# Making the low halves of a weight slab at the end of VectorE's round in the attention of a two-block network

## The chip, the cores and the metric

The kernel runs on one core of a Trainium2 chip. The metric is the time of one execution on the device in microseconds (us), the median of several runs.

## The reference, cut to what matters

Ten layers over 256 tokens of width 1024: feed-forward layers, a mixer, a short convolution, a shared key and value projection and a sparse attention. All is float32. Only the mixer is touched:

```
h = x @ w_in                      # 1024 -> 3 * 3 * 384 (q, k, v of three branches) + 3 * 1024 (gates)
o_m = moba_attention(...)         # 6 heads, one block here: causal softmax with ALiBi
o_d = diff_attention(...)         # 6 heads, softmax_1 - lam * softmax_2, then RMSNorm per head
o_s = stick_breaking_attention(...)   # 6 heads
gates = sigmoid(g + b_gate)
merged = gates_0 * (o_m @ w_br_moba) + gates_1 * (o_d @ w_br_diff) + gates_2 * (o_s @ w_br_sb)
out = merged @ w_out
```

## The kernel before, in words

**Slabs.** Every weight matrix comes through SBUF in slabs of 128 x 2048 float32 (1 MB; some of the mixer's are 128 x 1536) in a ring of four slots. A float32 product is made of three float32r matmuls (`product`, L1566 to L1568), so each slab is split: ScalarE copies `raw` to the rounded high half `w_hi` (L628), VectorE subtracts it from `raw` and so makes the low half `w_lo` (L974). A slab's high half waits until its load has landed and TensorE has used the slab four before it (`slab_used`); its low half waits for the high half (`high_ready`); TensorE waits for the low half (`low_ready`), and so does the load into the same slot of the slab four further on (SyncE's queue, L394).

**The mixer.** Its 36 slabs are numbered 0 to 35 here. Slabs 0 to 31 are those of 19 tiles (`TILES`), one or two slabs each. The tiles are pieces of q, k and v, six half gates (for each branch two of 512 columns) and six half branch products. Tile number t accumulates in the PSUM banks of pair t mod 2 (`pair_of`). Before TensorE begins a tile, it waits until all earlier tiles of that pair were read out (`pair_read`). The tiles that matter below: tile 6 is the second half of the first gate (slabs 12, 13), tiles 7 and 8 the first branch's products (slabs 14 and 15), tiles 9 and 10 queries, keys and values of the third branch (slabs 16 to 19), tiles 11 and 12 the second gate (20 to 23), tiles 13 and 14 the second branch's products (24 and 25), tile 15 half of the third gate (26, 27).

**Rounds.** The attention of the 18 heads (u = 0 to 17, six to a branch) is woven between the slabs by a table written out by hand; `ROUND[i]` holds the slabs of round i:

```
STEPS = [6] + [1] * 8 + [2] * 3 + [1] * 4 + [2, 1, 1] + [4]
```

So round 7 has slab 12, round 8 slab 13, round 9 slabs 14 and 15, round 10 slabs 16 and 17, round 11 slabs 18 and 19, rounds 12 to 15 slabs 20 to 23, round 16 slabs 24 and 25, rounds 17 and 18 slabs 26 and 27, round 19 the last four. Each engine runs its own loop over u in the order of its program, and in pass u works on round u + 1:

- TensorE: the slabs of round u + 1; the square sums of a pair of heads (L1817, odd passes of the second branch); the three transposes of the weights of head u (L1790, waits `prob_ready`); the scores of a head ahead; the output of head u - 1 (L1810 to L1812), which for an even u - 1 also waits until the pair of heads before it was taken out of its bank, by VectorE's L1191 or L1206.
- ScalarE: reads out q and k tiles, copies the transposed weights (L726), exponentials of head u + 1 (L717; in the third branch a logarithm chain L697 to L709), the high half of a finished pair of heads (L734), the four sigmoids of a gate whose second half was made in this round, with a table load on either side (L689, L690), and last the high halves (L628) of the slabs four after those of round u + 1.
- VectorE: reads out the round's tiles (`tiles`: v L1103, gates L1113, branch products L1125 or L1128 and L1129, each tile ended by a nop at L1115 or L1131 that counts `pair_read`), the root mean square's sum (L1191), the maxima of head u + 1 (L1144 to L1154), the weights of head u + 1 (L1174 to L1183, in the third branch L1164 to L1169), the low half of a finished pair of heads (L1206), the pair's normalisation (L1197 to L1201), and the low halves L974 of slabs.

The branch products at L1125 and L1128 multiply by the gate, so VectorE waits there for ScalarE's sigmoids (`gated`).

Of the kernel before, what the change touches and what calls it, by code (L numbers as in the profile page):

```python
# [54 lines left out]
def two_block_kernel(nc, t, out):  # L55
# [5 lines left out]
    with ExitStack() as ctx:  # L61
# [246 lines left out]
        HEADS = BRANCH_HEADS  # L308
# [17 lines left out]
        ROUND = [range(sum(STEPS[:i]), sum(STEPS[:i + 1])) for i in range(len(STEPS))]  # L326
# [60 lines left out]
        def _(sp):  # L387
# [40 lines left out]
            for n, kind in enumerate(phases):  # L428
# [33 lines left out]
                elif kind == MIXER:  # L462
                    w = t["w_in"][0]
                    for d, (tile, kh) in enumerate(MIX_SLABS):
                        what = TILES[tile]
                        if d == ROUND[0].stop:
                            gains(n)

                            sp.wait_ge(normed, normed_before(n))
                            sp.dma_start(b_gate[:], t["b_gate"][0].partition_broadcast(P)).then_inc(loaded_mix, 16)  # L470
                        if what[0] == "gate":
                            c0 = GATE0 + what[1] * D + what[2] * 512
                            load(s0 + d, columns(w, kh, [(c0, 256), (c0 + 256, 256)]))
                        elif what[0] == "branch":
                            wb = t[("w_br_moba", "w_br_diff", "w_br_sb")[what[1]]][0]
                            src = wb[:, what[2] * 512:(what[2] + 1) * 512].rearrange("(k p) n -> p k n", p=P)

                            def pieces(slot):
                                dst = raw[:, slot, 0:BC * 512].rearrange("p (k n) -> p k n", k=BC)
                                return [(dst[:, :, 0:256], src[:, :, 0:256]), (dst[:, :, 256:512], src[:, :, 256:512])]  # L480
                            load(s0 + d, pieces)
                        else:
                            spans = QKV[what[0]][0]
                            load(s0 + d, columns(w, kh, spans, sum(c for _, c in spans)))
# [134 lines left out]
        def _(act):  # L619
# [41 lines left out]
            for n, kind in enumerate(phases):  # L661
                s0 = first_slab[n]
                if kind == MIXER:
                    def tile_out(tile):

                        what = TILES[tile]
                        if what[0] in QKV:
                            _, blocks, first = QKV[what[0]]
                            act.wait_ge(slab_used, s0 + MIX_SLABS.index((tile, 1)) + 1)
                            for i in range(blocks // 2):  # L670
                                at, src = first + 2 * i, pair_of(tile)[i][:].rearrange("p (k m) -> p k m", k=2)
                                queries = min(2, max(0, 4 * BC + BC - at)) if at >= 4 * BC else 0
                                if 0 < queries < 2:
                                    nc.scalar.activation(qk[:, at:at + queries, :], src[:, 0:queries, :], ACT.Copy, scale=HD ** -0.5)
                                    at, src, queries = at + queries, src[:, queries:, :], 0

                                nc.scalar.activation(qk[:, at:first + 2 * i + 2, :], src, ACT.Copy,
                                                     scale=HD ** -0.5 if queries else 1.0).then_inc(pair_read[tile % 2], 1)
# [280 lines left out]
        def _(dve):  # L959
# [8 lines left out]
            def split(k, i=0):  # L968

                if k >= TOTAL:  # L970
                    return
                slot, width = k % SLOTS, width_of(k)
                dve.wait_ge(high_ready, k + 1 + 4 * i)
                nc.vector.tensor_tensor(w_lo[:, slot, 0:width], raw[:, slot, 0:width],  # L974
                                        w_hi[:, slot, 0:width].bitcast(F32), ALU.subtract).then_inc(low_ready, 1)
# [110 lines left out]
            for n, kind in enumerate(phases):  # L1086
                s0 = first_slab[n]
                if kind == MIXER:
# [44 lines left out]
                    def maxima_of(u):  # L1133

                        b, hd = u // HEADS, u % HEADS
                        dve.wait_ge(scored, u + 1)
                        if before(u) > 0:
                            dve.wait_ge(probT_psum, before(u))
                        scale = HD ** -0.5 if b == MOBA else DIFF_SCALE
                        slope = alibi_slope(2 * hd if b == MOBA else 2 * hd + 1)  # L1140
                        maps = 1 if b == MOBA else 2
                        for m in range(maps):
                            side = u % 2 if b == MOBA else m
                            ins = nc.vector.scalar_tensor_tensor(out=prob[:, side, :], in0=far[:], scalar=slope / scale,  # L1144
                                                                 in1=bank[4 + side][:, 0:BW], op0=ALU.mult, op1=ALU.add)
                        ins.then_inc(score_read, 1)
                        dve.wait_ge(score_read, u + 1)
                        mx = head_max[:, u % 2, 0:2 * maps]
                        for m in range(maps):
                            side = u % 2 if b == MOBA else m  # L1150
                            for i, at in enumerate((ROWS_A, ROWS_B)):
                                ins = nc.vector.tensor_reduce(head_max[:, u % 2, 2 * m + i:2 * m + i + 1], prob[:, side, at], AX.X, ALU.max)
                        step(ins)
                        nc.vector.tensor_scalar(mx, mx, -scale, None, ALU.mult).then_inc(neg_ready, 1)  # L1154
# [33 lines left out]
                    def pair_spread(p):  # L1188

                        dve.wait_ge(o_sums, p - BC + 1)  # L1190
                        nc.vector.tensor_scalar(ms_d, bank[7][:, S:2 * S], 1.0 / HD, SUBLN_EPS, ALU.mult, ALU.add).then_inc(o_spread, 1)  # L1191

                    def pair_norm(p):

                        near_one = tmp[:, 0:S]
                        dve.wait_ge(o_rstd, p - BC + 1)
                        step(nc.vector.tensor_tensor(near_one, o_root, o_root, ALU.mult))  # L1197
                        step(nc.vector.tensor_tensor(near_one, near_one, ms_d, ALU.mult))
                        step(nc.vector.tensor_scalar(near_one, near_one, -0.5, 1.5, ALU.mult, ALU.add))
                        step(nc.vector.tensor_tensor(near_one, near_one, o_root, ALU.mult))  # L1200
                        nc.vector.scalar_tensor_tensor(out=o_f, in0=o_f, scalar=out_gain, in1=near_one,  # L1201
                                                       op0=ALU.mult, op1=ALU.mult).then_inc(o_normed, 1)

                    def pair_out(p, src):
                        dve.wait_ge(oT_high, p + 1)
                        nc.vector.tensor_tensor(oT_lo[:, p % BC, :], src, oT_hi[:, p % BC, :].bitcast(F32), ALU.subtract)\  # L1206
                            .then_inc(oT_ready, 1)

                    def tiles(i):
                        for d in ROUND[i]:  # L1210
                            if ends(d) is not None:
                                tile_out(ends(d))

                    def slabs(steps):
                        for d in steps:
                            split(s0 + d + 4)
# [8 lines left out]
                    for u in range(3 * HEADS):  # L1225

                        delayed = (u - 3) // 2 if u % 2 == 1 and (u - 3) // 2 // BC == DIFF else None
                        tiles(u + 1)
                        if delayed is not None:
                            pair_spread(delayed)  # L1230
                        if u + 1 < 2 * HEADS:
                            maxima_of(u + 1)
                        if u > 0:
                            slabs(ROUND[u][:1])
                        if u + 1 < 3 * HEADS:
                            weights_of(u + 1)
                        if u > 0:
                            slabs(ROUND[u][1:])
                        if u % 2 == 0 and u > 0 and (u // 2 - 1) // BC != DIFF:
                            pair_out(u // 2 - 1, bank[7][:, 0:S])  # L1240
                        if delayed is not None:
                            pair_norm(delayed)
                            pair_out(delayed, o_f)
                    slabs(ROUND[3 * HEADS])
                    pair_out(3 * BC - 1, bank[7][:, 0:S])
                    for d in ROUND[-1]:
                        if ends(d) is not None:
# [823 lines left out]
```

## Time and profile before

| | |
|---|---|
| time, median of 3 runs | 1755.72 us (1755.58 to 1756.56) |
| the profiled execution's own time | 1758.67 us |
| its span, first to last instruction | 1757.0 us |
| mean granted TensorE clock | 0.972 |
| busy: TensorE / VectorE / ScalarE | 96% / 55% / 43% |
| the mixer's rounds in the trace | 245 to 445 us |

A timeline is read line by line: start in us, duration in us, engine, line, operation, tensor written and read, count of like instructions merged, and in brackets the idle time of that engine just ahead of it with what ended it. Matmuls overlap, so the work of TensorE is measured from start to start.

### The profile page before, as it was taken

The page shows a single profiled execution, that of the slowest core. Times are in us where ns is not written, and L with a number is a line of the kernel's source. Part 1 is how long each engine was busy: PE and PEld are TensorE (multiplying, and loading weights), DVE is VectorE, ACT ScalarE, POOL GpSimd, SP SyncE. Part 2 cuts the span into 40 slices and gives each one's busy share as a digit, 9 for nine tenths or more (in the row PEclk, how much of TensorE's full clock was granted, in tenths as well). Part 3 has the DMA queues.
Part 4 walks back from the last instruction along what each step waited for, and adds up shares of the span by engine and source line. Part 5 has one row for each costly group of instructions (what it writes and reads, how often), then busy time and mean ns, then how long its engine had stood idle before and what let it go on. Part 6 is the DMA issues. An engine that isn't in the chain of part 4 may idle for free.

```text
span 1757.0 us, 21254 instructions
## 1 busy us (share of the span) xinstructions
PE 1683.7 (96%) x8310; PEld 1408.4 (80%) x8310; DVE 971.9 (55%) x1016; ACT 755.1 (43%) x914; POOL 44.3 (3%) x56
## 2 busy tenths in 40 slices
PE   7999999898799998999999999989999998999999
PEld 6888797776678886888799888878888887888887
DVE  5554557575565546554466655457555455555542
ACT  4554344545244433443334444336444344444431
POOL 1000100000010000000000000001000010000000
PEclk9999999998899999999999999999999988899999
DMA  9565563343356653665456565546565541036551
GB/s 289 170 212 192 173 205 115 96 146 135 127 168 190 218 186 109 219 196 184 158 180 192 168 191 199 184 157 206 177 195 190 168 167 43 1 96 206 180 188 48
DMA packets 226072, 290.88 MB, mean 166 GB/s; under 512 B 10516, under 2 KB 203728, under 8 KB 225872
## 3 DMA queue, kind: packets, MB, share of 16 engines
q1 hardware_dynamic: 226000, 289.87, 50.6%
q8 instruction: 51, 0.84, 0.2%
q14 instruction: 21, 0.17, 0.0%
HBM read 288.78 MB, written 1.05 MB: 165 GB/s over the span
## 4 chain that ended last, share of the span: by engine, by line
PE 90%; DVE 6%; ACT 2%; issue 1%; POOL 1%; DMA 0%; DVEq 0%; ACTq 0%
PE bank L1566 28%; PE bank L1568 27%; PE bank L1567 27%; DVE w_lo L974 2%; PE bank L1679 2%; PE bank L1991 1%; PE bank L1575 1%; PE bank L1966 1%; PE bank L1976 1%; DVE x_sb L995 1%; DVE xT_lo L980 1%; ACT w_hi L628 1%; ACT xT_hi L634 0%; PE bank L2006 0%; DVE xc_lo L1320 0%
## 5 line engine op out<-in xcount | busy, mean ns | idle before, releaser
L974 DVE TENSOR_TENSOR w_lo<-raw,w_hi 128x2048 fp32r<-128x2048 f32 x268 | 612.2, 2289 | 391.2 <-ACT w_hi L628 390.1
L628 ACT ACTIVATE w_hi<-raw 128x2048 fp32r<-128x2048 f32 x268 | 507.7, 1901 | 262.2 <-PE bank L1568 256.4
L1566 PE MATMUL bank<-w_hi,xT_lo 128*128 128x512 f32 (+1 forms) x1328 | 532.8, 401 | 30.1 <-DVE xT_lo L980 17.3
L1568 PE MATMUL bank<-w_hi,xT_hi 128*128 128x512 f32 (+1 forms) x1328 | 522.5, 393 | 0.0
L1567 PE MATMUL bank<-w_lo,xT_hi 128*128 128x512 f32 (+1 forms) x1328 | 521.9, 393 | 0.0
L1566 PEld LDWEIGHTS bank<-w_hi,xT_lo 128*128 128x128 f32 x1328 | 254.6, 192 | 84.9 <-DVE xT_lo L980 20.1
L1568 PEld LDWEIGHTS bank<-w_hi,xT_hi 128*128 128x128 f32 x1328 | 253.9, 191 | 53.9
L1567 PEld LDWEIGHTS bank<-w_lo,xT_hi 128*128 128x128 f32 x1328 | 254.7, 192 | 49.5
L1566 PE MATMUL bank<-w_hi,hT_lo 128*128 128x512 f32 x528 | 209.0, 396 | 0.0
L1568 PE MATMUL bank<-w_hi,hT_hi 128*128 128x512 f32 x528 | 208.4, 395 | 0.0
L1567 PE MATMUL bank<-w_lo,hT_hi 128*128 128x512 f32 x528 | 208.4, 395 | 0.0
L925 ACT ACTIVATE hT_hi<-bank 128x512 f32 (+1 forms) x66 | 39.4, 597 | 187.0 <-PE bank L1679 186.9
L1568 PEld LDWEIGHTS bank<-w_hi,hT_hi 128*128 128x128 f32 x528 | 99.3, 188 | 23.7
L1567 PEld LDWEIGHTS bank<-w_lo,hT_hi 128*128 128x128 f32 x528 | 99.4, 188 | 23.3
L1566 PEld LDWEIGHTS bank<-w_hi,hT_lo 128*128 128x128 f32 x528 | 99.3, 188 | 23.3
L937 ACT ACTIVATE silu<-bank 128x256 f32<-128x256 f32 x132 | 43.5, 382 | 172.2 <-PE bank L1568 172.1
L1566 PE MATMUL bank<-xT_hi,w_lo 128*128 128x256 f32 x368 | 107.3, 292 | 6.8 <-DVE w_lo L974 4.0
L1567 PE MATMUL bank<-xT_lo,w_hi 128*128 128x256 f32 x368 | 106.4, 289 | 0.0
L1568 PE MATMUL bank<-xT_hi,w_hi 128*128 128x256 f32 x368 | 106.3, 289 | 0.0
L1515 DVE TENSOR_TENSOR hT_lo<-bank,hT_hi 128x512 f32 (+1 forms) x66 | 45.6, 691 | 106.6 <-ACT hT_hi L925 106.5
L1526 DVE TENSOR_TENSOR h<-silu,bank 128x256 f32<-128x256 f32 x132 | 49.6, 418 | 68.5 <-ACT silu L937 68.5
L1566 PEld LDWEIGHTS bank<-xT_hi,w_lo 128*128 128x128 f32 x368 | 73.0, 198 | 8.8 <-issue 5.0
(247 smaller groups left out, 1259.3 us busy)
## 6 DMA issues: line engine op xcount, KB each, us to landing
raw<-in_ffn_w_gate_up_dram SPq DMA_DIRECT2D x176, 512.0 KB, 4.7
raw<-in_ffn_w_down_dram SPq DMA_DIRECT2D x132, 512.0 KB, 4.2
raw<-in_ffn_w_gate_dram SPq DMA_DIRECT2D x44, 512.0 KB, 4.0
raw<-in_ffn_w_up_dram SPq DMA_DIRECT2D x44, 512.0 KB, 5.0
raw<-in_w_in_dram SPq DMA_DIRECT2D x44, 512.0 KB, 4.8
raw<-in_conv_w_in_dram SPq DMA_DIRECT2D x24, 512.0 KB, 4.5
raw<-in_kv_w_dram SPq DMA_DIRECT2D x12, 512.0 KB, 4.3
raw<-in_w_out_dram SPq DMA_DIRECT2D x8, 512.0 KB, 4.8
```

Source lines behind the costliest of these rows:

```text
L628: nc.scalar.activation(w_hi[:, slot, 0:width], raw[:, slot, 0:width], ACT.Copy).then_inc(high_ready, 1)
L925: nc.scalar.activation(hT_hi[:, bass.ds(2 * j + 4 * i, 2), :], bank[4 + j % 2][:].rearrange("p (c m) -> p c m", c=2), ACT.Copy).then_inc(h ...
L937: nc.scalar.activation(silu[:, tt, :], bank[2 * (j % 2) + tt][:, 0:256], ACT.Silu).then_inc(silu_ready, 1)
L974: nc.vector.tensor_tensor(w_lo[:, slot, 0:width], raw[:, slot, 0:width], w_hi[:, slot, 0:width].bitcast(F32), ALU.subtract).then_inc(low_r ...
L980: nc.vector.tensor_tensor(xT_lo[:, 4 * q:4 * q + 4, tt * P:(tt + 1) * P], src[:].rearrange("p (k m) -> p k m", k=4), xT_hi[:, 4 * q:4 * q ...
L995: ins = nc.vector.scalar_tensor_tensor(out=part, in0=Y[tt][half][:], scalar=factor, in1=part, op0=ALU.mult, op1=ALU.add)
L1515: nc.vector.tensor_tensor(hT_lo[:, bass.ds(2 * j + 4 * i, 2), :], bank[4 + j % 2][:].rearrange("p (c m) -> p c m", c=2), hT_hi[:, bass.ds( ...
L1526: nc.vector.tensor_tensor(h[:, tt, :], silu[:, tt, :], bank[2 * (j % 2) + tt][:, 256:512], ALU.mult).then_inc(h_ready, 1)
L1566: nc.tensor.matmul(o, x_lo, wh, start=first, stop=False, skip_group_check=shared)
L1567: nc.tensor.matmul(o, x_hi, wl, start=False, stop=False, skip_group_check=shared)
L1568: return nc.tensor.matmul(o, x_hi, wh, start=False, stop=last_one, skip_group_check=shared)
L1679: ins = nc.tensor.transpose(dst[:, c, tt * P:(tt + 1) * P], h[:, tt, c * P:(c + 1) * P], ident[:])
```

## The change

VectorE's low halves move within its loop. Before, pass u made the low halves that belong to the round before its own: the first of them between the maxima and the weights of head u + 1, the others behind the weights. After, pass u makes all low halves of its own round, last in the pass. They are those of the slabs four after the round's. The other engines' programs are the same.

```diff
                         if u + 1 < 2 * HEADS:
                             maxima_of(u + 1)
-                        if u > 0:
-                            slabs(ROUND[u][:1])
                         if u + 1 < 3 * HEADS:
                             weights_of(u + 1)
-                        if u > 0:
-                            slabs(ROUND[u][1:])
                         if u % 2 == 0 and u > 0 and (u // 2 - 1) // BC != DIFF:
                             pair_out(u // 2 - 1, bank[7][:, 0:S])
                         if delayed is not None:
                             pair_norm(delayed)
                             pair_out(delayed, o_f)
-                    slabs(ROUND[3 * HEADS])
+                        slabs(ROUND[u + 1])
                     pair_out(3 * BC - 1, bank[7][:, 0:S])
```

## Rows read from the trace of the kernel before

**Rows 1.** The page: busy time of each engine, and the chain that ended last

```profile
PE 1683.7 (96%) x8310; PEld 1408.4 (80%) x8310; DVE 971.9 (55%) x1016; ACT 755.1 (43%) x914; POOL 44.3 (3%) x56
...
PE 90%; DVE 6%; ACT 2%; issue 1%; POOL 1%; DMA 0%; DVEq 0%; ACTq 0%
```

**Rows 2.** Timeline of TensorE in the mixer's rounds

```profile
311.69 0.49 PE L1790 MATMUL bank<-ident,prob 128*128 128x128 f32 x3
...
313.77 0.39 PE L1566 MATMUL bank<-xT_hi,w_lo 128*128 128x256 f32 x1
...
325.38 0.59 PE L1817 MATMUL bank<-o_norm,same_head 128*128 128x256 f32 x2
...
331.94 0.55 PE L1566 MATMUL bank<-xT_hi,w_lo 128*128 128x256 f32 x1 [3.99 <-DVE w_lo L974]
...
345.98 0.49 PE L1790 MATMUL bank<-ident,prob 128*128 128x128 f32 x3
...
352.12 0.77 PE L1566 MATMUL bank<-w_hi,xT_lo 128*128 128x512 f32 x1 [3.99 <-DVE w_lo L974]
...
360.43 0.59 PE L1817 MATMUL bank<-o_norm,same_head 128*128 128x256 f32 x2
...
364.81 0.50 PE L1566 MATMUL bank<-w_hi,xT_lo 128*128 128x512 f32 x1
...
370.39 0.49 PE L1790 MATMUL bank<-ident,prob 128*128 128x128 f32 x3
...
404.40 0.80 PE L1566 MATMUL bank<-w_hi,xT_lo 128*128 128x512 f32 x1 [2.73 <-DVEq L1131]
...
420.59 0.55 PE L1790 MATMUL bank<-ident,prob 128*128 128x128 f32 x3 [1.22 <-ACT prob L709]
...
424.65 0.80 PE L1566 MATMUL bank<-w_hi,xT_lo 128*128 128x512 f32 x1
```

**Rows 3.** A stretch's busy time, granted clock (PEclk) and DMA, TensorE alone

```profile
352.10:357.00 4.90, 4.88 (x12) 0.50 0.50 161
...
424.70:429.00 4.30, 4.30 (x17) 0.82 0.92 324
```

**Rows 4.** Timeline of VectorE, passes 7 to 11 and 15

```profile
302.89 1.02 DVE L1144 SCALAR_TENSOR_TENSOR prob<-far,bank 128x384 f32<-128x384 f32 x2 [0.21 <-DVE gates L1113]
...
305.19 2.28 DVE L974 TENSOR_TENSOR w_lo<-raw,w_hi 128x2048 fp32r<-128x2048 f32 x1
307.39 0.17 DVE L1174 RECIPROCAL head_sum<-head_sum 128x4 f32<-128x4 f32 x1
...
309.26 1.28 DVE L1125 TENSOR_TENSOR z_sb<-gates,bank 128x512 f32<-128x512 f32 x2
...
327.22 1.02 DVE L1144 SCALAR_TENSOR_TENSOR prob<-far,bank 128x384 f32<-128x384 f32 x2 [0.71 <-PE bank L1781]
...
329.51 2.29 DVE L974 TENSOR_TENSOR w_lo<-raw,w_hi 128x2048 fp32r<-128x2048 f32 x1
...
361.06 0.42 DVE L1191 TENSOR_SCALAR o_norm<-bank 128x256 f32<-128x256 f32 x1 [5.04 <-PE bank L1817]
...
401.49 0.69 DVE L1128 TENSOR_TENSOR gates<-gates,bank 128x512 f32<-128x512 f32 x1 [1.50 <-ACT gates L689]
...
407.33 2.29 DVE L974 TENSOR_TENSOR w_lo<-raw,w_hi 128x2048 fp32r<-128x2048 f32 x1
```

**Rows 5.** Timeline of ScalarE, passes 7, 9 and 14

```profile
305.32 0.40 ACT L717 ACTIVATE prob<-prob,head_max 128x128 f32<-128x128 f32 x1 [3.16 <-DVE head_max L1154]
...
312.00 1.91 ACT L628 ACTIVATE w_hi<-raw 128x2048 fp32r<-128x2048 f32 x1
...
338.30 3.70 ACT L628 ACTIVATE w_hi<-raw 128x2048 fp32r<-128x2048 f32 x2
...
399.07 0.39 ACT L734 ACTIVATE oT_hi<-bank 128x256 fp32r<-128x256 f32 x1 [4.16 <-PE bank L1568]
...
404.27 1.91 ACT L628 ACTIVATE w_hi<-raw 128x2048 fp32r<-128x2048 f32 x1
```

## The prediction

> **What bounds the kernel now.** I read the page first: TensorE is busy 96% of the span and makes up 90% of the chain that ended last, VectorE is busy 55% [rows 1]. So the change can pay or cost only where TensorE waits. I then read TensorE's timeline through the mixer, with the idle times in brackets [rows 2]. Two waits of 3.99 us are put down to low halves: slab 18 began at 331.94 and slab 20 at 352.12 in place of 327.95 and 348.13. A third, 2.73 us ahead of slab 26 (404.40), is put down to VectorE's nop at L1131: TensorE waited until a bank pair was read out. A fourth, 1.22 us at 420.59, is a wait for the last head's weights. Last I read the timelines of VectorE and ScalarE around these places [rows 4, 5].
>
> A wait costs more than itself. Slab 20 ran at 0.50 of the clock, the 1.2 GHz level, for its first 4.9 us [rows 3]. It took 8.31 us (352.12 to 360.43) where slab 21 took 5.58 (364.81 to 370.39): 2.73 lost. Slabs 18 and 19 took 14.04 where 16 and 17 took 11.61 (313.77 to 325.38): 2.43 lost. Slab 26 loses about as much [rows 2].
>
> **The change, part by part.** Of the 22 low halves of passes 0 to 17 all but the last move. They are the same instructions, 2.20 us from start to start (305.19 to 307.39 [rows 4]), 1.67 by proportion of width for the narrow ones; nothing is added or removed. Each now stands at the end of a pass, where it waits for a high half that is the last thing ScalarE does in that pass. Behind it in VectorE's queue stand the next round's tile read-outs, the sum L1191 and the maxima. Loads follow low halves; these come earlier in most rounds, and where they come later (low halves 28 to 31, by 1 to 6 us) the slot's next high half is due ten and more us on, so I cost DMA at nothing. If that cover went, a load would cost its delay one to one.
>
> Passes 0 to 6: I walked them with the spacings of rows 4 and 5. The low half lands in VectorE's idle time or where the old one stood, the next maxima move by at most 3.3 us, and the weights stay ahead of their transposes. I take 0 for TensorE, at most 0.5. One shift matters: slab 16's low half now stands ahead of tile 6's read-out, so that read-out and the maxima behind it move by 2.2, the maxima from 302.89 to 305.1.
>
> *First new wait.* The exponentials follow the maxima by 2.43 us (305.32 against 302.89), and slab 17's high half follows the exponentials by 6.68 us (312.00), since the four sigmoids and two table loads lie between [rows 4, 5]. So it starts at 314.2 and ends at 316.15. Slab 17's low half, now last in pass 7, runs 316.15 to 318.35, and only then does VectorE read tile 7 (L1125, before at 309.26). Tile 7 and tile 9 share a bank pair, so slab 16 waits for that read: 318.35 + 1.28 + 0.18 for the nop = 319.8 in place of 313.77. **Loss 6.1**, and 2.4 of clock. The square sums come at 333.9 in place of 325.38.
>
> *The two old waits.* Low halves 18 and 19 are now made in pass 8. Its maxima begin at 321.3, its weights end at 327.4, high halves 18 and 19 run from 326.2 to 330, so the low halves are done at 330.4 and 332.6. Slab 18 is wanted 2.57 us after the square sums (325.38 to 327.95), at 336.4: no wait. It starts 4.5 later than before and runs at full clock, so the transposes of head 10 come at 348.05, 2.1 later than 345.98. Pass 9: the maxima move from 327.22 to 335.7. High halves 20 and 21 followed them by 11.08 us (338.30); 2.4 of that was low halves standing between and goes. They start at 344.3, and the low halves run 346.3 to 348.5 and 348.5 to 350.7. Slab 20 is wanted at 348.05 + 2.15 = 350.2: no wait, 1.7 us of margin. It starts 1.9 earlier than before, keeps its clock, and would end 4.65 earlier, at 355.8. So the two waits and their clock (3.99 + 2.43 + 3.99 + 2.73 = **13.1 gained**) turn the 8.5 lost into 4.6 ahead.
>
> *What is late next.* In pass 10 VectorE is in low half 21 until 350.7, reads the v tile (0.6), begins the maxima at 351.3 (before 347.39), and the weights are ready 2.43 + 1.9 (exponentials) + 1.8 (weights, 307.39 to 309.26) later, at 357.4; ScalarE's squares for the square sums are ready at 356.3. TensorE idles 0.6 and 0.7 us. Low halves 22 and 23 then wait for high halves 22 and 23, which begin at 356.2, and hold VectorE until 362.6. Behind them stands L1191 (before 361.06), which the output of head 10 needs, wanted at 360.7: another 2.3 us. Slab 21 starts at 363.85, only 1.0 earlier than 364.81. **Loss 3.6.** No row shows the clock after three such waits close together: the bounds are 0 and the 2.7 that slab 20 lost; I take 1.5, between them. Head 12's transposes are then 0.5 later than 370.39. Passes 12 and 13 hold this.
>
> *Second new wait.* The same pattern, in pass 14. High half 27 follows L734 by 5.20 us (399.07 to 404.27 [rows 5]), since the second gate's sigmoids lie between. With L734 at 399.6, low half 27 runs 406.75 to 408.95, and the second branch's products (L1128, before 401.49) start then. Slab 26 needs their bank pair: 408.95 + 2.73 + 0.18 = 411.9 in place of 404.40. **Loss 7.5**, less the 0.5 already counted; the clock loss is there before as well. Part comes back: before, low half 27 stood ahead of the next weights (407.33), and the 1.22 us wait at 420.59 and the waits with it go. With low halves 28 and 29 ahead of the last weights these are ready at 426.5, the transposes run at 426.7, and the last outputs wait some 0.5 for ScalarE's copy behind high half 30. Slab 28 starts at 429.5 in place of 424.65, +4.85. The clock loss that it had (4.3 us at 0.82, or 0.8 [rows 3]) may go: I take 0.7 off, +4.2. Behind slab 28 all is as before.
>
> Sum: 6.1 + 2.4 - 13.1 + 3.6 + 1.5 + 7.0 - 2.6 - 0.7 = **+4.2 us**. The profiled execution, 1758.67 (span 1757.0), would become 1762.9; it stands 2.95 above the median of the runs, so the forecast is 1755.72 + 4.2 = **1760.0**.
>
> The two new waits rest on VectorE doing its queue in order. In the trace low half 27 began at 407.33, behind the branch products, though high half 27 was ready at 404.27 + 1.91 = 406.2 [rows 4, 5]. The Trainium skill ("TensorE: Matmul & The Clock Gate", section on the array's architectural detail) says that ScalarE's and VectorE's queues are strictly first in, first out, while TensorE can only pull weight loads forward. By that rule the low half blocks the read-out and the sum is the one above; could VectorE pass over a waiting subtraction, it would be that of the first rival. No row here shows an engine passing over a waiting instruction.
>
> **The rivals.** *The bank pairs come back in time (faster).* Then only the 13.1 us of the two old waits count, and perhaps the loss of 3.6: 1742.6 to 1748. It decides at one point, high half 17: it would have to start by 308 for tile 7 to be read by 313.6, and it started at 312.00, behind the sigmoids. Similarly 27. Against it speak both rows; for it, only an error of mine in the pairs.
> *The gains and losses cancel (within 0.2%).* The sum has about 20 us of terms of either sign. With no clock loss at 364 and the first new wait 1 us shorter it gives +1.7, 1757.4. The trace allows it.
> *Slab 20 waits again (slower still).* The margin of 1.7 us ahead of slab 20 rests on the normalisation moving forward. If high halves 20 and 21 come 3 us later, slab 20 waits 1.3 and loses clock, 2.7: +8.2, 1763.9. With clock loss at each of the small waits, 1766.
> *The change does nothing (no change).* Most low halves do move only into other idle time; but then the waits at 331.94 and 352.12 would have to stay, and what made them late was VectorE's order alone: low half 18 stood in pass 9, behind that pass's maxima (327.22, then 329.51 [rows 4]).
>
> **How the numbers follow.** My case 0.66, its own range 1757.5 to 1763.5; cancelling 0.16; slab 20 waiting 0.10; bank pairs in time 0.06; nothing 0.02. 0.2% is 3.5 us, about what a measurement of this kernel can tell from no change. My case puts a tenth of all chance below +3.5. So slower 0.64, within 0.2% 0.28, faster 0.08. The range is 1755.0 to 1765.0; it leaves out the faster rival and the worst end.
>
> **What would show it.** TensorE's waits at slabs 18 and 20 are gone; slab 16 waits about 6 us and slab 26 about 9 to 10, both put down to L1131; output 10 waits for L1191; slab 28 starts 3 to 6 us later than 424.65. If slab 16 does not wait, the first step is wrong and the kernel is faster. If the rounds between 340 and 400 run later than before by over 3 us, the middle is mis-sized.

## The result, and the profile after

The changed kernel takes 1760.59 us (median, 1754.17 to 1764.93 over 12 runs) where the kernel before took 1756.65 in the same sessions (1750.42 to 1759.94). The ratio is 1.0027, 95% interval 1.0014 to 1.0040: slower, by 2.5 to 7 us. Forecast was +4.2 us.

The single profiled executions do not show this in their spans: 1757.0 before, 1756.6 after. The reading must be made in the stretch that the change touches. It begins with the first scores of the attention, in the kernel before here:

```profile
244.44 0.50 PE L1780 MATMUL bank<-qk 64*128 64x128 f32 x4 [1.22 <-issue]
```

and reaches to slab 28, at 424.65 [rows 2]: 180.2 us. Below it is called the stretch. TensorE's timeline in the changed kernel (its lines are numbered four lower):

```profile
245.25 0.50 PE L1776 MATMUL bank<-qk 64*128 64x128 f32 x4 [1.22 <-issue]
...
320.79 0.58 PE L1562 MATMUL bank<-xT_hi,w_lo 128*128 128x256 f32 x1 [6.03 <-DVEq L1131]
334.54 0.59 PE L1813 MATMUL bank<-o_norm,same_head 128*128 128x256 f32 x2
337.05 0.38 PE L1562 MATMUL bank<-xT_hi,w_lo 128*128 128x256 f32 x1
350.74 0.50 PE L1562 MATMUL bank<-w_hi,xT_lo 128*128 128x512 f32 x1
357.08 0.70 PE L1813 MATMUL bank<-o_norm,same_head 128*128 128x256 f32 x2 [0.57 <-ACT o_norm L745]
358.21 0.55 PE L1786 MATMUL bank<-ident,prob 128*128 128x128 f32 x3 [0.43 <-DVE prob L1183]
363.91 0.66 PE L1806 MATMUL bank<-probT,v_mix 128*64 128x128 f32 x2 [1.38 <-DVE o_norm L1191]
365.35 0.80 PE L1562 MATMUL bank<-w_hi,xT_lo 128*128 128x512 f32 x1
...
375.90 0.50 PE L1562 MATMUL bank<-w_hi,xT_lo 128*128 128x512 f32 x1
...
414.04 0.80 PE L1562 MATMUL bank<-w_hi,xT_lo 128*128 128x512 f32 x1 [9.65 <-DVEq L1131]
...
431.66 0.50 PE L1562 MATMUL bank<-w_hi,xT_lo 128*128 128x512 f32 x1
```

The two waits for low halves [rows 2] are gone: slabs 18 (337.05) and 20 (350.74) start without brackets. In their place stand 6.03 us ahead of slab 16 and 9.65 ahead of slab 26 (it was 2.73), both put down to the nop that ends a branch product's read-out, and three small waits around head 11. The stretch is 431.66 - 245.25 = 186.4 us, 6.2 longer. What hides this in the span lies elsewhere: the sparse attention, from VectorE's first add of the layer ahead of it to its own, lasted from 1414.57 to 1556.95 in this execution and from 1407.54 to 1557.31 in the one before, 7.4 us less, in a stage that the change does not touch. The granted clock of this stage was 0.90 here and 0.86 in the one before.

VectorE's queue around the first new wait:

```profile
311.39 0.75 DVE L1183 SCALAR_TENSOR_TENSOR prob<-prob,head_sum 128x128 f32<-128x128 f32 x2
317.12 2.29 DVE L974 TENSOR_TENSOR w_lo<-raw,w_hi 128x2048 fp32r<-128x2048 f32 x1 [4.98 <-ACT w_hi L628]
319.33 1.28 DVE L1125 TENSOR_TENSOR z_sb<-gates,bank 128x512 f32<-128x512 f32 x2
```

VectorE stands idle 4.98 us for high half 17, then makes the low half, and reads tile 7's product after it, at 319.33 (before 309.26 [rows 4]). ScalarE's rows say what the high half waited for:

```profile
311.61 2.19 ACT L689 ACTIVATE gates<-gates 128x512 f32<-128x512 f32 x4
313.82 1.28 ACT L690 ACT_TABLE_LOAD   x1
315.11 1.91 ACT L628 ACTIVATE w_hi<-raw 128x2048 fp32r<-128x2048 f32 x1
```

The sigmoids were done at 313.8. The product's read-out could have begun then; it was not at the head of its queue.

Around the second new wait VectorE's queue shows the same: 6.23 us idle for high half 27, the low half, and only then the branch product (before at 401.49 [rows 4]).

```profile
408.93 2.29 DVE L974 TENSOR_TENSOR w_lo<-raw,w_hi 128x2048 fp32r<-128x2048 f32 x1 [6.23 <-ACT w_hi L628]
411.13 0.68 DVE L1128 TENSOR_TENSOR gates<-gates,bank 128x512 f32<-128x512 f32 x1
```

The clock around the waits (columns: window, its length, TensorE busy, count, granted clock, DMA share, GB/s):

```profile
320.70:325.00 4.30, 4.21 (x19) 0.50 0.77 243
358.00:359.00 1.00, 0.79 (x5) 1.00 0.00 0
360.00:361.00 1.00, 1.00 (x6) 0.50 0.00 0
365.30:370.00 4.70, 4.70 (x12) 0.50 0.80 264
```

After the 6.03 us wait it is 0.50, the 1.2 GHz level. What had been left open, the small waits, brings it down too, and earlier than expected: it is 0.50 from 360 on, after the waits of 0.57 and 0.43 us and ahead of the third, and still is while slab 21 begins.

### The profile page after: what moved, and what is told of

It is laid out like the page before. It is cut to its first block, busy times and chain, and to the rows that moved or that the text cites. A ratio compares the mean times of both kernels' runs of the same rounds, so it can differ in the third digit from the quotient of the medians.

```text
span 1756.6 us, 21259 instructions
## 1 busy us (share of the span) xinstructions
PE 1677.9 (96%) x8310; PEld 1401.7 (80%) x8310; DVE 971.3 (55%) x1016; ACT 755.0 (43%) x914; POOL 44.3 (3%) x56
## 4 chain that ended last, share of the span: by engine, by line
PE 87%; DVE 7%; ACT 3%; issue 1%; POOL 1%; DMA 0%; SPq 0%; DVEq 0%; ACTq 0%
PE bank L1562 27%; PE bank L1564 26%; PE bank L1563 26%; DVE w_lo L974 2%; PE bank L1675 2%; PE bank L1962 1%; PE bank L1987 1%; ACT w_hi L628 1%; PE bank L1571 1%; PE bank L1972 1%; DVE x_sb L995 1%; DVE xT_lo L980 1%; ACT prob L717 0%; ACT xT_hi L634 0%; DMA raw<-in_ffn_w_up_dram 0%
## 5 line engine op out<-in xcount | busy, mean ns | idle before, releaser
L628 ACT ACTIVATE w_hi<-raw 128x2048 fp32r<-128x2048 f32 x268 | 507.6, 1901 | 261.5 <-PE bank L1564 255.3
L937 ACT ACTIVATE silu<-bank 128x256 f32<-128x256 f32 x132 | 43.5, 382 | 172.4 <-PE bank L1564 172.3
```

The source lines that it names most:

```text
L628: nc.scalar.activation(w_hi[:, slot, 0:width], raw[:, slot, 0:width], ACT.Copy).then_inc(high_ready, 1)
L937: nc.scalar.activation(silu[:, tt, :], bank[2 * (j % 2) + tt][:, 0:256], ACT.Silu).then_inc(silu_ready, 1)
```

## The experiments

All are timed against the kernel before on the same chip. The kernel before had medians of 1752.03 us beside the four kernels from "passes 7, 14 set back" to "high halves ahead of sigmoids", 1752.87 beside the next four and 1756.15 beside the last four, so rows are compared by ratio and not by median. The stretch comes from one execution of each, and moves by one to two us with the granted clock even where the waits are the same; the ratios of times carry the intervals. Most intervals of the faster versions overlap: they tell these versions from the kernel before, but hardly from one another, and such comparisons rest on the waits in the traces.

| kernel | stretch, us | wait at slab 16 / 18 / 20 / 26 | median, us | ratio to before (95%) |
|---|---|---|---|---|
| before | 180.2 | 0 / 3.99 / 3.99 / 2.73 | 1756.65 beside the changed one | 1 |
| changed | 186.4 | 6.03 / 0 / 0 / 9.65 | 1760.59 | 1.0027 (1.0014 to 1.0040) |
| passes 7, 14 set back | 172.7 | 0 / 0 / 0 / 2.73 | 1745.52 | 0.9958 (0.9945 to 0.9972) |
| pass 7 set back | 177.2 | 0 / 0 / 0 / 9.66 | 1750.58 | 0.9984 (0.9967 to 1.0001) |
| pass 14 set back | 181.5 | 6.04 / 0 / 0 / 2.73 | 1754.18 | 1.0008 (0.9995 to 1.0020) |
| high halves ahead of sigmoids | 173.2 | 1.11 / 0 / 0 / 4.74 | 1745.10 | 0.9970 (0.9952 to 0.9987) |
| both set back, sum first | 172.3 | 0 / 0 / 0 / 2.73 | 1746.50 | 0.9965 (0.9944 to 0.9985) |
| the same, last weights first | 170.6 | 0 / 0 / 0 / 2.73 | 1744.94 | 0.9954 (0.9933 to 0.9974) |
| the same, low half 21 later | 171.2 | 0 / 0 / 0 / 2.73 | 1740.91 | 0.9933 (0.9908 to 0.9958) |
| before, rounds 9 and 10 moved | 169.0 | 0 / 0 / 0 / 2.73 | 1740.96 | 0.9936 (0.9912 to 0.9961) |
| before, round 9 moved | 173.7 | 0 / 0 / 3.98 / 2.73 | 1744.89 | 0.9948 (0.9930 to 0.9965) |
| before, round 10 moved | 171.7 | 0 / 3.99 / 0 / 2.73 | 1750.55 | 0.9966 (0.9951 to 0.9982) |
| before, rounds 9, 10, 12, 13 moved | 172.8 | 0 / 0 / 0 / 2.74 | 1744.09 | 0.9945 (0.9920 to 0.9969) |
| before, low halves 18, 19, 20 moved | 167.1 | 0 / 0 / 0 / 2.74 | 1740.79 | 0.9911 (0.9885 to 0.9938) |

**Setting back the two passes with sigmoids.**

```diff
                             maxima_of(u + 1)
+                        if u - 1 in (7, 14):
+                            slabs(ROUND[u])
                         if u + 1 < 3 * HEADS:
                             weights_of(u + 1)
...
-                        slabs(ROUND[u + 1])
+                        if u not in (7, 14):
+                            slabs(ROUND[u + 1])
```

> The changed kernel, but in passes 7 and 14 (those with a gate's sigmoids) VectorE makes the low halves where the kernel before made them, in the next pass between maxima and weights. My theory (the loss is the read of tiles 7 and 13 behind a low half whose high half stands behind the sigmoids): TensorE's wait at slab 16 is gone, that at slab 26 shrinks from 9.65 to about 2.7 us, no wait on a low half at slabs 18 and 20; from the first scores to slab 28 some 171 to 174 us, where the kernel before took 180.2 and the changed one 186.4; the time is 6 to 9 us under the kernel before (ratio 0.995 to 0.997). Rival (the low half at the end of a pass costs in every round, sigmoids or not): the stretch stays above 180 us and the time at or above that of the kernel before.

The theory held on every number. TensorE's rows:

```profile
245.89 0.50 PE L1779 MATMUL bank<-qk 64*128 64x128 f32 x4 [1.22 <-issue]
...
315.34 0.39 PE L1565 MATMUL bank<-xT_hi,w_lo 128*128 128x256 f32 x1
...
329.46 0.38 PE L1565 MATMUL bank<-xT_hi,w_lo 128*128 128x256 f32 x1
...
356.32 0.66 PE L1809 MATMUL bank<-probT,v_mix 128*64 128x128 f32 x2 [2.42 <-DVE o_norm L1191]
...
398.77 0.79 PE L1565 MATMUL bank<-w_hi,xT_lo 128*128 128x512 f32 x1 [2.73 <-DVEq L1131]
...
418.58 0.50 PE L1565 MATMUL bank<-w_hi,xT_lo 128*128 128x512 f32 x1
```

Two low halves out of 22 turn a loss of 0.27% into a gain of 0.42%.

**One of the two at a time** (the tuple is `(7,)` or `(14,)`).

> The changed kernel with pass 7 alone set back. My theory: no wait at slab 16, the wait at slab 26 stays at 9 to 10 us; the stretch from the first scores to slab 28 is about 178 us (before 180.2, changed 186.4), the time 1 to 4 us under the kernel before. Rival (one blocked read-out matters, the other lies in slack): the stretch comes out within 1 us of that with both passes set back, or within 1 us of the changed kernel's.

> The changed kernel with pass 14 alone set back. My theory: slab 16 still waits 6.0 us, slab 26 waits 2.7 to 3 in place of 9.65; the stretch to slab 28 is 181 to 183 us, the time 1 to 3 us above the kernel before. Rival (the losses are not additive, what is saved at slab 26 comes back as a wait at heads 16 and 17): the stretch stays at 185 us or more.

Both held. From 186.4 us, pass 7 set back saves 9.2 us of the stretch and pass 14 saves 4.9; together they saved 13.7, so the two losses add. Both times have 1 inside the interval (0.9984 and 1.0008): the expected 1 to 4 us below and 1 to 3 us above the kernel before are not refuted, nor resolved.

**ScalarE's high halves ahead of its sigmoids, in the changed kernel.**

```diff
-                        tiles(u + 1, sigmoids)
                         slabs(u + 1)
+                        tiles(u + 1, sigmoids)
```

> The changed kernel, with ScalarE making the round's high halves ahead of the sigmoids in place of behind them. My theory (high half 17 and 27 are late only because of the sigmoids and their two table loads, 4.8 us): slab 16 waits 1 to 2 us in place of 6.0, since the sigmoids now come 1.9 us later; slab 26 waits about 5 in place of 9.65; the stretch to slab 28 is 176 to 180 us, and the time within 3 us of the kernel before. Rival (the low half itself, or VectorE's own backlog, makes the read-out late): slab 16 waits over 4 us.

The rows carry the cause:

```profile
313.75 0.38 PE L1562 MATMUL bank<-xT_hi,w_lo 128*128 128x256 f32 x1 [1.11 <-DVEq L1131]
...
398.67 0.80 PE L1562 MATMUL bank<-w_hi,xT_lo 128*128 128x512 f32 x1 [4.74 <-DVEq L1131]
```

VectorE's order is the changed one; only the other queue differs, and the waits fall to 1.11 and 4.74. So it is not the low half's place alone that costs, but that place together with a high half behind the sigmoids. The stretch, 173.2, is shorter than the 176 to 180 expected, and the time, 0.997 of before, is some 5 us under it where 3 was the bound (the interval reaches from 2 to 8 us): I had not counted that with a wait of 1.11 us slabs 16 and 17 keep their clock (11.6 us for the two).

**VectorE's sum ahead of low halves 22 and 23** (on top of both passes set back).

```diff
-                        if delayed is not None:
+                        if delayed is not None and u != 11:
                             pair_spread(delayed)
...
+                        if u == 10:
+                            pair_spread(4)
                         if u not in (7, 14):
                             slabs(ROUND[u + 1])
```

> The kernel with passes 7 and 14 set back, and in pass 10 VectorE does the sum L1191 ahead of low halves 22 and 23. My theory (the output of head 10 waits 2.4 us only because L1191 stands behind two low halves): that wait is gone, slab 21 starts about 3 us earlier against the first scores (before this edit 111.9 us after them), the stretch to slab 28 is 168 to 170.5 us where it was 172.7, the time 9 to 12 us under the kernel before. Rival (the clock falls all the same, or the logarithm chain of head 12 is late next): slab 21 starts earlier, but the stretch stays at 171.5 us or more.

The wait of 2.42 us is gone and slab 21 starts 2.3 us earlier (109.5 after the first scores), but the stretch is 172.3 in place of 172.7, and the time 0.9965 of before, no gain on 0.9958 and some 6 us under the kernel before where 9 to 12 were expected: the rival held. Its VectorE rows show where it went:

```profile
350.84 4.49 DVE L974 TENSOR_TENSOR w_lo<-raw,w_hi 128x2048 fp32r<-128x2048 f32 x2 [0.25 <-ACT w_hi L628]
355.25 0.55 DVE L1164 SCALAR_TENSOR_TENSOR tmp<-bank,prob 128x384 f32<-128x384 f32 x1
...
370.94 1.76 DVE L974 TENSOR_TENSOR w_lo<-raw,w_hi 128x1536 fp32r<-128x1536 f32 x1 [2.76 <-ACT w_hi L628]
372.62 0.41 DVE L1191 TENSOR_SCALAR o_norm<-bank 128x256 f32<-128x256 f32 x1
```

Low half 25 leaves VectorE idle 2.76 us, and the next sum stands behind it, at 372.62; head 12's output waited 0.97 us for it, and slab 23 ran slow behind that wait.

**Two more on this line.** Low halves 28 and 29 behind the last head's weights in pass 16, then also low half 21 in pass 10 between maxima and weights:

```diff
+                        if u == 16:
+                            slabs(ROUND[u])
...
-                        if u not in (7, 14):
+                        if u not in (7, 14, 15):
                             slabs(ROUND[u + 1])
```

```diff
+                        if u == 10:
+                            slabs(ROUND[u][1:])
                         if u + 1 < 3 * HEADS:
                             weights_of(u + 1)
...
+                        if u == 9:
+                            slabs(ROUND[u + 1][:1])
-                        if u not in (7, 14, 15):
+                        elif u not in (7, 14, 15):
                             slabs(ROUND[u + 1])
```

> The last kernel with the sum first, and low halves 28 and 29 moved from the end of pass 15 to pass 16, behind the weights and the finished pair. Theory: the wait for the last head's weights, 2.04 us with both passes set back, falls to some 1.2 us, bounded by ScalarE's logarithms behind its two high halves; the stretch shortens by 0.5 to 1 us. Rival (the low halves then hold up the read-out of tile 15 and slab 30): the stretch does not change or grows.

The last head's wait fell from 2.04 to 1.29. The stretch is 1.6 shorter, of which 0.5 lies behind slab 24, where the edit is. The rest is not the edit's: in this execution slab 21 started 0.8 us later, the 0.97 us wait at head 12 did not occur, and slab 23 took 5.6 us in place of 6.9.

> The last kernel, and low half 21 alone moved from the end of pass 9 to pass 10 beside the exponentials. Theory (head 11's maxima are late because VectorE is in low half 21): the two waits of 0.57 and 0.43 us at the square sums and transposes of head 11 go, the stretch to slab 28 is 1 to 2 us shorter than that of the last kernel, 165.5 to 168.5 us. Rival (slab 21's half comes late, or low halves 22 and 23 slip by as much): no shorter.

The two waits at head 11 went and slab 21 came 2.3 us earlier than in the sum-first kernel. Yet the stretch was not shorter, 171.2 against 170.6: 1.23 us at the next pair's square sums (put down to ScalarE's squares) and 0.76 at head 12's output appeared, and slab 23 ran slow behind them. The rival held for the stretch. The ratios, 0.9933 and 0.9954, do not tell the two kernels apart.

**The kernel before with four low halves moved.**

```diff
-                        if u > 0:
+                        if u > 0 and u not in (9, 10):
                             slabs(ROUND[u][:1])
...
-                        if u > 0:
+                        if u > 0 and u not in (9, 10):
                             slabs(ROUND[u][1:])
...
+                        if u in (8, 9):
+                            slabs(ROUND[u + 1])
                     slabs(ROUND[3 * HEADS])
```

> The kernel before, with the low halves of rounds 9 and 10 alone (slabs 18 to 21) made at the end of their own pass, all others where they were. My theory (the whole gain of the change lies in these four low halves): no wait on a low half at slabs 18 and 20, slab 16 does not wait, head 10's output does not wait for L1191, slab 26 waits 2.7 us as before; the stretch from the first scores to slab 28 is 168 to 170 us in place of 180.2, the time 9 to 13 us under the kernel before. Rival (the earlier low halves of the other rounds carry part of the gain): the stretch is above 172 us.

It held: 169.0 us, 11.2 under the kernel before. So four of the low halves make the whole gain, and all the others together cost 186.4 - 169.0 = 17.4 us of the stretch. Some two of these may be the clock's luck: behind the same waits of 0.57 and 0.43 us at head 11 it stayed at 1.00 here and fell to 0.50 in the changed kernel. Its VectorE rows beside those of the kernel with the sum first:

```profile
348.27 2.29 DVE L974 TENSOR_TENSOR w_lo<-raw,w_hi 128x2048 fp32r<-128x2048 f32 x1 [0.25 <-ACT w_hi L628]
351.94 0.56 DVE L1164 SCALAR_TENSOR_TENSOR tmp<-bank,prob 128x384 f32<-128x384 f32 x1 [1.37 <-ACT prob L701]
352.53 1.01 DVE L1167 TENSOR_TENSOR_SCAN far<-tmp 128x128 f32<-128x128 f32 x2
353.57 0.56 DVE L1169 TENSOR_TENSOR prob<-bank,far 128x384 f32<-128x384 f32 x1
354.16 2.29 DVE L974 TENSOR_TENSOR w_lo<-raw,w_hi 128x2048 fp32r<-128x2048 f32 x1
```

One low half stands on either side of the weights, in time that is idle anyway. With both ahead of them the weights began 4.4 us after the first low half; here 3.7, and the second costs nothing.

**Each of the two rounds alone** (`(9,)` or `(10,)`).

> The kernel before with the low halves of round 9 alone (slabs 18 and 19) made at the end of their own pass. Theory (the two old waits are separate; each has its own late low half): slab 18 does not wait, slab 20 still waits 3.99 us for low half 20, which stands between the maxima and weights of the next pass; the stretch from the first scores to slab 28 is 173 to 175 us (before 180.2, both rounds moved 169.0). Rival (the second wait follows from the first): slab 20 waits under 2 us and the stretch is under 171.

> The kernel before with the low halves of round 10 alone (slabs 20 and 21) made at the end of their own pass. Theory: slab 18 waits 3.99 us as before, slab 20 does not wait, and the waits at head 11's square sums and transposes do not appear, since round 11's slabs run late enough; slab 21 starts 114 us after the first scores (before 120.4), the stretch is 173 to 175 us. Rival (low halves 20 and 21 ahead of the v tile's read-out and the maxima cost whatever the state of TensorE): head 11 waits 1 us or more and the stretch is above 175.5.

The two old waits are separate: with round 9 alone slab 20 still waits 3.98, with round 10 alone slab 18 waits 3.99. With round 10 alone no wait appeared at head 11. Its stretch, 171.7, is below the 173 to 175 expected. Slabs 18 and 19 lost less to the clock after the same wait (13.0 us where the kernel before took 14.04 [rows 2]).

**Rounds 12 and 13 too** (`(9, 10, 12, 13)`).

> The kernel before with rounds 9, 10, 12 and 13 moved (slabs 18 to 21, 24 and 25). Theory (in the third branch a low half at the end of a pass waits for a high half that stands behind ScalarE's L709, and holds up L1191 and the next weights; that is where the gain of the sum-first version went): the output of head 12 waits for L1191, the stretch is 170 to 172 us where rounds 9 and 10 alone gave 169.0. Rival (a low half there fits into idle time; round 11 alone did the harm): the stretch stays within 0.5 us of 169.0.

The theory held in kind, by more than expected: 172.8, or 3.7 above 169.0.

```profile
367.46 0.70 PE L1819 MATMUL bank<-o_norm,same_head 128*128 128x256 f32 x2 [1.32 <-ACT o_norm L745]
...
371.12 0.66 PE L1812 MATMUL bank<-probT,v_mix 128*64 128x128 f32 x2 [0.74 <-DVE o_norm L1191]
372.57 0.80 PE L1568 MATMUL bank<-w_hi,xT_lo 128*128 128x512 f32 x1
```

Behind them slab 23 took 7.3 us in place of 5.6. These are the waits that the sum-first versions met (0.97 at the output; 1.23 and 0.76 with low half 21 later), so rounds 12 and 13 suffice for them.

**Three low halves moved, the fourth beside the exponentials.**

```diff
+                        if u == 10:
+                            slabs(ROUND[u][1:])
...
+                        if u + 1 in (9, 10):
+                            slabs(ROUND[u + 1][:1] if u == 9 else ROUND[u + 1])
```

> The kernel before with low halves 18, 19 and 20 at the end of their own pass and low half 21 one pass on, between the maxima and weights of head 11. Theory: the waits of 0.57 and 0.43 us at head 11 go, nothing else appears, the stretch is 167.5 to 168.5 us, against 169.0 with all four at the end. Rival (the 1 us is given back at the square sums two rounds on, which wait for ScalarE): 169.0 or more.

The waits at head 11 went and no new wait took their place: 167.1 us, a little under the 167.5 to 168.5 expected and the shortest stretch of all. Part of the lead over the kernel with all four at the end is given back just behind the stretch: slabs 28 and 29 took 13.0 us here and 11.7 there, so that slab 30 starts 180.2 us after the first scores against 180.7. The time is 0.9911 of before (0.9885 to 0.9938), which does not tell it from the 0.9936 of that kernel.

## Why the prediction was right, step by step

Set against the first scores of each trace, so that what lies ahead of them drops out:

| start of | predicted | measured |
|---|---|---|
| slab 16 | 75.4 | 75.5 |
| slab 18 | 92.0 | 91.8 |
| slab 20 | 105.8 | 105.5 |
| slab 21 | 119.4 | 120.1 |
| slab 26 | 167.5 | 168.8 |
| slab 28 | 185.1 | 186.4 |

- *First new wait*, 6.1 and 2.4 of clock (the forecast's own terms, 319.8 - 313.77, give 6.0): measured 6.03, and slabs 16 and 17 took 13.75 us where they took 11.61 [rows 2], 2.1 lost. The runs with pass 7 set back and with the high halves first show the cause.
- *The two old waits*, 13.1 gained: both went, and each alone brings back its own wait.
- *What is late next*, 3.6 and 1.5 of clock: right in its waits, too small in its clock. The waits were 0.57, 0.43 and 1.38 us, 2.4 in all. VectorE came to L1191 when the forecast had it, 118.1 us after the first scores; the third wait was shorter than 2.3 because the clock had fallen ahead of it, and the small matmuls of head 11 ran 2.1 us longer. Slab 21 then took 2.2 us longer than its 5.58. So the clock took 4.3 us, not 1.5, and more than the 2.7 that the forecast had as its upper bound, since that bound counted one slab and not the small matmuls ahead of it. In sum this is 1.6 us more than forecast. It makes the 1.3 us by which slab 28 is late, for slab 20 had come 0.3 early. That L1191 is held up by low halves 22 and 23 is shown by the run with the sum first.
- *Second new wait*, 7.5 later: slab 26 waits 9.65, as the forecast's 9 to 10 had it.
- *Part comes back*, 2.6, and 0.7 of clock: slab 26 to slab 28 took 17.6 us where it took 20.25, and slabs 28 and 29 took 11.0 where they took 11.8. So slab 30 starts 5.4 us later than before, against the first scores, where +4.2 was forecast. The medians differ by 3.9 us and the ratio by 4.7; with an interval of 2.5 to 7 us the times cannot tell 4.2 from 5.4, and that the medians lie so near the forecast is in part luck.
- *Loads* at nothing: held. In the changed kernel's trace no high half of the mixer waits for its load; the one wait ahead of L628 from 245 to 450 us, 5.0 us, is put down to TensorE.
- *The low halves of passes 0 to 6* at nothing, at most 0.5: slab 14 starts at 304.14 (before 303.22), 0.1 later against the first scores. Held. (A narrow low half is 1.65 us by proportion, not 1.67; nothing hangs on it.)
- *Passes 12 and 13 hold this* was true of the sum but hid a price. There the forecast compared the changed kernel with a kernel before that had itself been delayed. Where the earlier waits are taken away, the low halves at the end of these passes cost 3.7 us more than in their old place.

The rival in which bank pairs come back in time did not occur in the changed kernel. Setting back passes 7 and 14 shows what it would have been worth: 172.7 us, 7.5 under the kernel before, not 13.1. The part missing, 5.6, is mainly what is late next: in that run the waits at head 11 are 0.57, 0.43 and 2.42 us, and the matmuls behind them ran some 2.5 us longer.

## What to carry to other kernels

An item moved to the end of a queue's round takes with it the wait for whatever the other engine does last in that round; before moving it, ask what stands behind it, and above all who waits for a bank to be read out. A uniform rule over all rounds added gains of 11 us and losses of 17 here; the two waits for low halves in TensorE's timeline named the two rounds whose four low halves were worth moving. Where a change within a few tenths of a per cent is to be read, compare a fixed stretch of the trace and not the spans, and let it reach past the last slab that a wait can slow down.

## What the runs showed of the hardware that was not expected

- The granted clock fell to 0.50 without any long gap: in the changed kernel it was 1.00 at 358 to 359 us and 0.50 at 360 to 361, with only the waits of 0.57 and 0.43 us at head 11 ahead of it, and slab 21 ran at 0.50 from 365.3 to 370.0. Behind the same two waits it fell as well in the two kernels with the sum first whose low half 21 stays in pass 9, without a third wait, and stayed at 1.00 in the kernel before with rounds 9 and 10, or 9, 10, 12 and 13, moved. What decides it is not shown. In the kernel with three low halves moved, slabs 28 and 29 took 13.0 us (411.43 to 424.46, where the same two took 11.0 in the changed one), behind waits of 1.25 and 1.65 us.
- The cost of one and the same wait differs between executions: slabs 18 and 19 took 14.04 us in one and 13.0 in another behind 3.99 us, and slab 26 took 7.4 us behind 9.65 in the changed kernel and 8.5 behind 9.66 with pass 7 set back.
- Whole runs of one kernel spread over nearly 10 us (1750.42 to 1759.94 before), with 7.4 us of difference seen in one stage whose program is the same.
